# Attention scores right behind the transposed probabilities of the preceding batch, in a two-layer hybrid decoder trunk on one Trainium2 core

## The reference

```
h = rms_norm(x); z = h @ w_in                        # 2048 -> 5384 columns, cut among three mixers
y_attn  = sliding-window (128) attention, 16 query heads, 2 kv heads, head dim 64, rotary, sinks
y_hgrn  = HGRN2 gated linear recurrence, 4 heads, 128x128 state, RMSNorm, silu gate
y_mlstm = mLSTM matrix memory, 4 heads, causal conv of width 4 ahead of it, sigmoid gate
x = x + concat(y_attn, y_hgrn, y_mlstm) @ w_out
x = x + PEER(rms_norm(x))     # 8 heads pick 16 of 16384 experts per token; rows of u and v are gathered
```

```
logits = q @ k.T / 8, masked to the window; the head's sink is one more logit without a value
p = softmax([logits, sink])[..., :-1]; y = p @ v
```

## Time and profile before

| | us |
|---|---|
| median of 3 runs | 3664.84 (3664.51 to 3666.08) |
| profiled execution, its own time | 3669.12 |
| its span, first to last instruction | 3667.2 |
| TensorE busy | 2884.9 (79%) |
| VectorE busy | 2199.1 (60%) |
| ScalarE busy | 755.4 (21%) |
| GpSimd busy | 1381.4 (38%) |

### The profile page before, as it was taken

One profiled execution on the slowest core, in us unless ns is written; L12 is line 12 of the kernel. 1 busy time (PEld: TensorE's weight loads), 2 busy tenths in 40 slices (PEclk: granted clock), 3 DMA queues, 4 the chain that ended last, 5 costly groups with the idle time before them and its releaser, 6 DMA issues.

```text
span 3667.2 us, 33187 instructions
## 1 busy us (share of the span) xinstructions
PE 2884.9 (79%) x10443; PEld 1674.5 (46%) x10443; DVE 2199.1 (60%) x3066; ACT 755.4 (21%) x1171; POOL 1381.4 (38%) x1028
## 2 busy tenths in 40 slices
PE   7999928877787788777789999288777877887776
PEld 7887814433342343332288778144333423433322
DVE  6665576565655566655466655756656655665655
ACT  4344401111111111110043444011111111111100
POOL 0000055554545455544300000555455454555542
PEclk9999969999999999999989999699999999999999
DMA  5434579999999999999944344799999999999998
GB/s 188 144 133 149 184 277 411 412 413 402 406 419 419 388 419 419 421 415 410 381 151 138 127 155 167 296 410 415 417 409 406 420 417 389 418 420 421 415 416 352
DMA packets 239376, 1244.02 MB, mean 339 GB/s; under 512 B 24632, under 2 KB 32896, under 8 KB 106880
## 3 DMA queue, kind: packets, MB, share of 16 engines
q0 software_dynamic: 147456, 1073.81, 71.2%
q1 hardware_dynamic: 91776, 168.51, 13.5%
HBM read 1240.14 MB, written 2.10 MB: 339 GB/s over the span
## 4 chain that ended last, share of the span: by engine, by line
DMA 33%; PE 29%; DVE 19%; issue 11%; DVEq 3%; POOL 3%; ACT 2%; POOLq 0%; ACTq 0%; SPq 0%
DMA work<-in_peer_v_dram,idx_v 19%; PE PS L470 15%; DMA work<-in_peer_u_dram,idx_u 14%; PE PS L762 12%; DVE work L1617 6%; POOL work L1078 3%; DVE xs L1630 2%; DVE lo L1202 1%; ACT hi L836 1%; DVE gain L1561 1%; DVEq L1293 1%; DVE gain L1562 1%; ACT work L890 1%; DVE gain L1595 1%; DVE gain L1564 0%
## 5 line engine op out<-in xcount | busy, mean ns | idle before, releaser
L762 PE MATMUL PS<-work,diag 128*128 128x512 f32 x3968 | 1862.1, 618 | 645.1 <-DMA work<-in_peer_v_dram,idx_v 439.8
L1617 DVE CUSTOM_DVE_ANT_0 work<-work,hn 128x2048 f32<-128x2048 f32 x512 | 1164.1, 2291 | 868.2 <-DMA work<-in_peer_u_dram,idx_u 826.0
L762 PEld LDWEIGHTS PS<-work,diag 128*128 128x128 f32 x3968 | 745.0, 196 | 1734.4 <-issue 1338.1
L1078 POOL DMA_INDIRECT work<-in_peer_u_dram,idx_u x512 | 755.7, 1476 | 1547.9 <-issue 606.0
L1078 POOL DMA_INDIRECT work<-in_peer_v_dram,idx_v x512 | 625.5, 1222 | 704.4 <-PE PS L762 583.8
L1027 ACT ACTIVATE diag<-cst,act_k 128x128 f32<-128x128 f32 x496 | 189.6, 398 | 1406.2 <-PE PS L762 1393.9
L470 PE MATMUL PS<-hT_hi,hi 128*128 128x256 f32 x1024 | 309.9, 303 | 49.4 <-DVE lo L1515 26.2
L470 PE MATMUL PS<-hT_lo,hi 128*128 128x256 f32 x1024 | 298.7, 292 | 0.0
L470 PE MATMUL PS<-hT_hi,lo 128*128 128x256 f32 x1024 | 298.1, 291 | 0.0
L470 PE MATMUL PS<-hi,hT_hi 128*128 128x512 f32 (+1 forms) x704 | 278.0, 395 | 13.1 <-DVE lo L1202 5.2
L470 PE MATMUL PS<-lo,hT_hi 128*128 128x512 f32 (+1 forms) x704 | 272.1, 386 | 0.0
(11 more groups left out here) (240 smaller groups left out, 1600.0 us busy)
## 6 DMA issues: line engine op xcount, KB each, us to landing
raw<-in_w_in_dram SPq DMA_DIRECT2D x40, 1024.0 KB, 5.0
gain<-in_w_in_dram SPq DMA_DIRECT2D x40, 1024.0 KB, 5.0
raw<-in_peer_query_dram SPq DMA_DIRECT2D x24, 1024.0 KB
raw<-in_w_out_dram SPq DMA_DIRECT2D x16, 1024.0 KB, 5.1
gain<-in_w_out_dram SPq DMA_DIRECT2D x16, 1024.0 KB, 5.1
work<-in_peer_query_dram SPq DMA_DIRECT2D x8, 1024.0 KB, 7.4
work<-in_peer_u_dram,idx_u POOLq DMA_INDIRECT x512
work<-in_peer_v_dram,idx_v POOLq DMA_INDIRECT x512
```

The costliest lines, as they stand in the source:

```text
L762: mm = pe.matmul(PS[:, j, :], diag[:, n % RING, :], vrow[n % RING][:, j * 512:(j + 1) * 512], start=(k == 0), stop=(k == (TOPK - 2 if last ...
L1078: pool.indirect_dma_start(out=dst, out_offset=None, in_=tables[table], in_offset=bass.IndirectOffsetOnAxis(ap=idx, axis=0)).then_inc(loade ...
L1617: dve.tensor_tensor_reduce(r, r, hn[:, b, :], 1.0, 0.0, ALU.mult, ALU.add, pre[:, b, k:k + 1]).then_inc(u_free.sem, 1)
```

## The change

`scores(n+1)` moves from behind piece 26+2n (there after `attend(n)`) to behind piece 25+2n, right after `turn_probs(n)`. `attend(n)` stands alone behind piece 26+2n. On VectorE `take_probs(n)` and `soft(n+1)` come before the convolution's quarter and `take_attended(n)`, every `split_to` of these functions takes one piece less, and `soft(n)` waits also for the transposes of batch n-1, as it overwrites `probs`. On ScalarE a `round_to(28+2n)` stands between the exponentials and the wait for the transposes, and `drain(6)` moves ahead of `batch_exps(3)`.

```diff
-                def batch_step(n):
+                def probs_step(n):
                     def go():
-                        if n > 0:
-                            attend(n - 1)
-                        if n < NBATCH:
-                            scores(n)
+                        turn_probs(n)
+                        if n + 1 < NBATCH:
+                            scores(n + 1)
                     return go
...
-                for n in range(NBATCH + 1):
-                    steps[24 + 2 * n] = batch_step(n)
-                    if n < NBATCH:
-                        steps[25 + 2 * n] = lambda n=n: turn_probs(n)
+                steps[24] = lambda: scores(0)
+                for n in range(NBATCH):
+                    steps[25 + 2 * n] = probs_step(n)
+                    steps[26 + 2 * n] = lambda n=n: attend(n)
...
                     a.then_inc(exped.sem, 1)
+                    round_to(28 + 2 * n)
                     act.wait_ge(probs_turned.sem, probs_turned.upto(l, n + 1))
...
                 batch_exps(1)
                 batch_exps(2)
+                drain(6)
                 batch_exps(3)
-                drain(6)
                 batch_exps(4)
...
# soft(n)
-                    split_to(27 + 2 * n)
+                    split_to(26 + 2 * n)
                     dve.wait_ge(scored.sem, scored.upto(l, n + 1))
+                    if n > 0:
+
+                        dve.wait_ge(probs_turned.sem, probs_turned.upto(l, n))
...
# take_probs(n)
-                    split_to(28 + 2 * n)
+                    split_to(27 + 2 * n)
...
# take_attended(n)
-                    split_to(29 + 2 * n)
+                    split_to(28 + 2 * n)
...
+                soft(0)
                 for n in range(NBATCH):
-                    soft(n)
+                    take_probs(n)
+                    if n + 1 < NBATCH:
+                        soft(n + 1)
                     if 1 <= n < 5:
                         convolve(n - 1)
-                    take_probs(n)
                     take_attended(n)
```

## The result

| | before | changed |
|---|---|---|
| median us (runs) | 3665.46 (4: 3664.51 to 3666.87) | 3632.05 (4: 3628.21 to 3637.51) |
| profiled execution, its span | 3669.12, 3667.2 | 3630.5, 3628.6 |

A fourth run of the kernel before puts its median at 3665.46, where the forecast started from 3664.84. The kernel is faster by 33.4 us where 19.9 were forecast. The range of 3639 to 3656 missed it from above. The mechanism that I described is there, and about 24 us of the gain are its; some 9 to 10 us came from a place that the prediction held to be untouched.

The account below looks back on a forecast made before the run. TensorE with its weight pieces was taken as the bound around the attention batches; its stops, 9.43 x 2 = 18.9 us, plus 1.0 of clock give 19.9, so 3664.84 becomes 3645, range 3639 to 3656.

Parts of the forecast that it names:

- What bounds the kernel: Around the attention batches TensorE with its weight pieces is the bound; its stops give away 9.43 us a layer.
- the chain of each stop: TensorE's stops in the attention stage traced to late exponentials, drain and lo through the VectorE and ScalarE queues.
- six stops: TensorE idles per layer: 0.89, 0.65, 1.86, 2.21 before turn_probs, 2.10 before piece 32, 1.27 before piece 37.
- the walk: Part-by-part timing of one new attention period over the engines' queues, 15.0 us long.
- Step 1: TensorE's order: five scores groups a layer one piece earlier; period 15.00 us, cost taken as 0, bound -0.3 to +0.3.
- Step 2: VectorE's order and new wait for probs_turned in the attention batches: wait already met, 0 us; splits have margins 4.9 and 7.
- The rivals: Exponentials stay late, 3657, 0.06; clock falls each period, 3666, 0.06; late weights, 3705, 0.04; edit doesn't bind, excluded.
- step 7: Way out of the attention stage: the 1.27 stop before piece 37 goes, mLSTM chain's margin about 2, remainder shifts.
- Steps 3 to 5: ScalarE's exponentials early, margin 6 to 7; weights in time, margins 5 to 6; batch 0's idle of 0.89 goes.
- T: End of piece 25+2n on TensorE, from which one new period is timed, up to T+15.0.
- Step 6: drain(6) ahead of batch_exps(3) on ScalarE: the stop of 2.10 before piece 32 goes, 2.36 with its edges.
- Clock: TensorE's clock losses behind the second layer's stage, 3.4 us in all; a third, 1.0, taken as gain.

Follow-up runs that it names:

- e1: Kernel before plus only VectorE's five added waits for the preceding batch's transposes: 3657.51 us against 3668.15, ratio 0.9973.
- e5: Kernel before plus five VectorE drain instructions directly ahead of its loop over the expert heads: 3657.26 us against 3665.46, ratio 0.9976.
- e7: Changed kernel with the two memsets of each convolution quarter made one, four VectorE instructions fewer ahead of the loop: 3641.5 us, ratio 0.9935 to the kernel before.
- e10: Changed kernel with the split of piece 26 ahead of soft(0) again: 3635.67 us.
- e11: Changed kernel without the added round_to(28+2n) on ScalarE: 3633.32 us.
- e2: Kernel before with only drain(6) moved ahead of batch_exps(3): 3659.11 us against 3668.15, ratio 0.9976.
- e3: Changed kernel with drain(6) moved back behind batch_exps(3): 3637.54 us.
- e9: Changed kernel run again, unedited, on another occasion: 3630.17 us.
- e12: Changed kernel with the expert-head loops written out on TensorE, ScalarE, VectorE and GpSimd: 3623.79 us, ratio 0.9879 to the kernel before.
- e4: Changed queues of VectorE and ScalarE with TensorE's old order, scores(n+1) behind attend(n): 3671.37 us, ratio 1.0011 to the kernel before.
- e8: Changed kernel with only VectorE's loop over the expert heads written out: 3621.16 us, ratio 0.9881 to the kernel before.

## Why the prediction was wrong, point by point

- *What bounds the kernel, and the chain of each stop*: right. All six stops a layer are gone, in both layers, and the walk's times held within 0.3 us. From the first scores to piece 37 it takes 90.05 where "about 91" was said.
- *Step 1, TensorE's order*, "I ... take 0": mis-sized by a little. The new period is 14.89, not 15.00, and the stage won 10.4 in the first layer where 9.43 was said. The bound of -0.3 to +0.3 a period held it.
- *Step 2, the new wait*, "0 us": this is the step that failed. It was costed as a wait only. It also brings five instructions into VectorE's code, and the loop behind them moves off the place of the second stop: 8 to 11 us (e1 10.6, e5 8.2, e7 9.4). "The change touches nothing outside that part" and, in step 7, "the whole remainder shifts" fell with it. The rivals held no such case. In the trace of before the stop was to be seen (2.56 of "issue" behind 6.31), had I looked behind VectorE's jumps.
- *Steps 3 to 5*: right in the main. A load landed a little later than said: in the period shown ScalarE waits 0.36 us for a piece and rounds it from T+8.4, where the piece was to be there at T+7.4; TensorE doesn't wait for it. e10 gives the stop of 0.89 of batch 0 by itself. e11 shows the added rounding is needed in the last period only.
- *Step 6, drain(6)*: its stop went, but its worth hangs on the rest: 1.9 a layer alone in the old order (e2), 1.1 in the new one (e3), not 2.36. In the sum this did no harm, since the sum counted periods and not edits.
- *Step 7*: right up to the mixers' end; the chain behind `spread_m` stopped nothing.
- *Clock*: 1.0 was taken, and in the profiles compared it was 3.2 (107.56 - 106.01 = 1.6 in the stage's last pieces, 47.35 - 45.72 = 1.6 behind). By e9, which lost 1.6 in its first layer, and e12, which lost it in both, this is in part chance.
- *The rivals*: none of the three came. TensorE's clock stood at 1.00 through the stage though transposes and scores now stand together.

The account: e7 has the whole change except the loop's place, and is 24.0 below the kernel before: 10.4 twice from the stage, 3.2 of clock. That the clock's share, read from one profile of each, closes this sum of medians to the tenth is luck. The loop's place gives the other 9.4 to 33.4. Without it the forecast of 3645 would have been 3.5 too high, and in its range.

## What to carry to other kernels

An instruction added or removed ahead of a loop moves the loop's code, and here its place behind a jump was worth 9.4 us beside the 24.0 of the edit that was meant: look at the first instructions behind each jump for idle time without a releaser, and control a small change with the same number of instructions that do nothing. Where an engine that feeds transfers jumps back a few times only, write its loop out. Here it paid to put the work that feeds a product a whole period ahead of it, but the queues needed the consumer's move (e4): the reordered queues alone were 20 us a stage worse than with the new order.

## What the runs showed of the hardware that I had not expected

- A jump back of VectorE's loop over the heads (428 instructions from branch to branch) leaves it idle for 6.0 to 6.3 us, and for 2.3 to 2.6 more behind the first dot product, depending on where the loop's code stands; one instruction of shift moves that second stop by one instruction (e7). Its jump at the end of the first layer was cheaper, 2.9 us from the branch to the next instruction against 5.4 to 5.7 in the loop (kernel before); why is open.
- Of the 6 us of such a stop, 2.7 show in the total (10.9 by four, e8), in a stretch with a DMA share of 1.00.
- The same stretch of products without idle time took 45.72, 47.35 or 48.90 us at a granted clock of 1.00, 0.96 or 0.93, and two executions of one kernel differed in it (changed kernel and e9, first layer).
